# Prompt attention in a hybrid decoder step: a narrow reciprocal with copies that spread it, the scale folded into the query norm, a negated maximum, and the small units' transposes copied out by VectorE

## What is computed

```python
MLA_HEADS, MLA_NOPE, MLA_ROPE, MLA_V = 8, 64, 32, 64
MLA_SCALE = (MLA_NOPE + MLA_ROPE) ** -0.5

def _attn_block(q_lat, q_pe, q_pos, ckv, kpe, k_pos):
    s = einsum('bqhl,bkl->bhqk', q_lat, ckv) + einsum('bqhr,bkr->bhqk', q_pe, kpe)
    mask = (k_pos[None, :] <= q_pos[:, None])[None, None]
    s = where(mask, s * MLA_SCALE, NEG_INF)
    p = softmax(s, axis=-1)
    return einsum('bhqk,bkl->bqhl', p, ckv)

# in _mla_mixer
q = (_rmsnorm(cq, q_norm_g) @ w_qb).reshape(bsz, s, MLA_HEADS, MLA_NOPE + MLA_ROPE)
o = einsum('bshl,lhv->bshv', o_lat, w_uv)
```

## Time and profile before

| | |
|---|---|
| median of three runs | 3233.49 us |
| the profiled execution's own time | 3230.6 us |
| its span | 3228.9 us |
| TensorE matmul busy | 3012.1 us, 93% |
| VectorE busy | 1803.4 us, 56% |
| ScalarE busy | 944.1 us, 29% |
| mean granted TensorE clock | 0.956 |

### The profile page before, as it was taken

How to read it: one execution, slowest core, us unless ns; L and a number is a source line. 1 busy time by engine, 2 the same in 40 slices (tenths; PEclk the granted TensorE clock), 3 DMA queues, 4 the chain that set the end, 5 groups by cost and what they waited for, 6 DMA issues and landing times. The chain is left out here.

```text
span 3228.9 us, 51409 instructions
## 1 busy us (share of the span) xinstructions
PE 3012.1 (93%) x21202; PEld 2666.1 (83%) x21202; DVE 1803.4 (56%) x2982; ACT 944.1 (29%) x1550; POOL 244.4 (8%) x280
## 2 busy tenths in 40 slices
PE   6987888998999999999989779889999999999998
PEld 5975565668999999999989545556699999999998
DVE  4856677553454545444565757765535545444554
ACT  4034454553311111111220445445423111111113
POOL 2000001540000000000020000024200000000000
PEclk8986999998999999999989879999999999999998
DMA  4122102762111111111031310047421112111211
GB/s 104 46 38 55 22 5 66 252 210 68 33 53 40 51 49 53 47 40 40 23 55 34 65 39 8 11 138 236 156 62 40 54 46 58 42 40 40 59 32 67
DMA packets 226585, 207.97 MB, mean 64 GB/s; under 512 B 50260, under 2 KB 195796, under 8 KB 226148
## 3 DMA queue, kind: packets, MB, share of 16 engines
q1 hardware_dynamic: 200744, 119.38, 13.7%
q0 software_dynamic: 25600, 85.11, 8.5%
HBM read 193.58 MB, written 11.05 MB: 63 GB/s over the span
## 5 line engine op out<-in xcount | busy, mean ns | idle before, releaser
L189 PE MATMUL ps<-streamH,upH 128*128 128x344 f32 x2112 | 449.0, 321 | 6.5 <-issue 3.7
L189 PE MATMUL ps<-streamH,upL 128*128 128x344 f32 x2112 | 447.3, 320 | 0.0
L189 PE MATMUL ps<-streamL,upH 128*128 128x344 f32 x2112 | 445.9, 319 | 0.0
L2279 ACT ACTIVATE upH<-hc 128x1024 fp32r<-128x1024 f32 x88 | 93.4, 1061 | 967.9 <-PE ps L189 967.9
L189 PEld LDWEIGHTS ps<-streamH,upH 128*128 128x128 f32 x2112 | 354.4, 188 | 8.8 <-issue 4.9
L189 PEld LDWEIGHTS ps<-streamH,upL 128*128 128x128 f32 x2112 | 355.9, 188 | 0.0
L189 PEld LDWEIGHTS ps<-streamL,upH 128*128 128x128 f32 x2112 | 352.8, 188 | 0.0
L2443 DVE TENSOR_TENSOR xT<-xT,ps 128x1032 f32<-128x1032 f32 x176 | 216.0, 1228 | 227.6 <-PE ps L189 227.6
L443 PE MATMUL ps<-inH,inW 128*128 128x344 f32 (+1 forms) x1248 | 233.4, 323 | 31.3 <-DVE inW L497 31.3
L2404 DVE TENSOR_TENSOR hc<-ps,rstd 128x1032 f32<-128x1032 f32 x44 | 54.2, 1232 | 370.9 <-PE ps L189 370.9
L443 PEld LDWEIGHTS ps<-inH,inW 128*128 128x128 f32 (+1 forms) x1248 | 198.4, 183 | 38.5 <-DVE inW L497 32.3
(11 more groups left out here) (475 smaller groups left out, 4787.2 us busy)
## 6 DMA issues: line engine op xcount, KB each, us to landing
hc<-in_w_ffn_in SPq DMA_DIRECT2D x88, 512.0 KB, 4.0
hc<-in_w_ffn_out SPq DMA_DIRECT2D x44, 512.0 KB, 3.7
big<-in_w_in SPq DMA_DIRECT2D x22, 512.0 KB, 4.0
stream_raw<-in_w_out SPq DMA_DIRECT2D x16, 512.0 KB, 4.0
big<-in_x_prompt SPq DMA_DIRECT2D x2, 2048.0 KB, 10.0
out_y_prompt<-big SPq DMA_DIRECT2D x8, 512.0 KB
scratch_y<-hc SPq DMA_DIRECT2D x16, 136.0 KB, 3.4
scratch_u<-wring SPq DMA_DIRECT2D x4, 516.0 KB, 3.1
```

The costliest lines, as they stand in the source:

```text
L189: last = pe.matmul(self.ps[:, bank + n, 0:NCOL], w, x[:, n * NCOL:(n + 1) * NCOL], start=(k == 0 and i == 0), stop=(k == len(terms) - 1 an ...
L2279: act.activation(upH[u][:, :, :], raw[u], ACT.Copy).then_inc(g_wh[u], 1)
```

## The change

- `reciprocals` runs once per group of four units. It takes the reciprocal of four row sums (128x4), then spreads the four columns with two copies into 128x128 blocks, two of which now alternate between groups. It stands at the third unit of the group. ScalarE's exponential no longer waits for the reciprocal of four units before.
- The scale is folded into the reciprocal root of the query norm, as a bias of log(scale) in that Exp, so that the exponentials run without a scale. In the sample stage the factor is -1.0 instead of minus the scale.
- The row maximum is written negated, and the instruction that scaled it is gone.
- The one bank of each small unit is copied out by VectorE and no longer by ScalarE, at its true width (128 to 512 columns).
- In VectorE's loop the copy of a unit now stands ahead of `output`; it stood behind it.

```diff
+                dve.memset(self.small[:, 21:22], math.log(MLA_SCALE))
...
-        rden = [take(P) for _ in range(2)]
+        rden = [take(2 * P) for _ in range(2)]
...
-        copied_by = ["DA"[g] if u % 2 == 0 else "A" for u in range(NU) for g in range(banks_of[u])]
+        copied_by = ["DA"[g] for u in range(NU) for g in range(banks_of[u])]
...
-                    pe.wait_ge(e_r, 4 * i + 4)
+                    pe.wait_ge(e_r, i + 1)
                     for w in range(2):
-                        pe.transpose(ps[:, VALUES_BANK, (2 * w + 1) * P:(2 * w + 2) * P], rden[w], ident)
+                        pe.transpose(ps[:, VALUES_BANK, (2 * w + 1) * P:(2 * w + 2) * P], rden[i % 2][:, w * P:(w + 1) * P], ident)
...
-                    act.activation(r, r, ACT.Exp, scale=-0.5).then_inc(d_rs, 1)
+                    act.activation(r, r, ACT.Exp, scale=-0.5, bias=self.small[:, 21:22] if i else 0.0).then_inc(d_rs, 1)
...
-                    if u >= 4:
-                        act.wait_ge(e_r, u - 3)
+                    if u >= 8:
+                        act.wait_ge(e_r, u // 4 - 1)
...
-                    s.link(dve.reduce_max(slot(2, u), two[:, 0:n], AX))
                     if u >= 4:
                         dve.wait_ge(e_p, u - 3)
-                    TS(slot(0, u), slot(2, u), -MLA_SCALE, None, ALU.mult).then_inc(e_nb, 1)
-
-                def reciprocals(u):
-                    p, z, q = units[u]
-                    dve.wait_ge(e_p, u + 1)
-                    if u // 4:
-                        dve.wait_ge(e_o, u // 4)
-                    dve.reciprocal(rden[1 - u % 2][:, 64 * z:64 * z + 64], slot(1, u).to_broadcast([P, 64])).then_inc(e_r, 1)
+                    dve.reduce_max(bound(u), two[:, 0:n], AX, negate=True).then_inc(e_nb, 1)
+
+                def reciprocals(i):
+                    dve.wait_ge(e_p, 4 * i + 4)
+                    s.link(dve.reciprocal(inverse, st[:, 4 + 4 * (i % 2):8 + 4 * (i % 2)]))
+                    if i >= 2:
+                        dve.wait_ge(e_o, i - 1)
+                    for w in range(2):
+                        last = dve.tensor_copy(rden[i % 2][:, w * P:(w + 1) * P].rearrange("p (z c) -> p z c", z=2),
+                                               inverse[:, 1 - w:4 - w:2].unsqueeze(2).to_broadcast([P, 2, 64]))
+                    last.then_inc(e_r, 1)
...
-                    dve.tensor_copy(pT[1][units[u][1]][:, 0:512], ps[:, 5 + at % 2, :]).then_inc(e_te, 1)
+                    w = min(4, units[u][2] + 1) * P
+                    dve.tensor_copy(pT[1 - u % 2][units[u][1]][:, 0:w], ps[:, 5 + at % 2, 0:w]).then_inc(e_te, 1)
...
                 for u in range(NU):
                     p, v = u // NV, u % NV
+                    copies(u)
                     if u and u % 4 == 0:
                         output(u // 4 - 1)
-                    if u % 2 == 0:
-                        copies(u)
-                    reciprocals(u)
+                    if u % 4 == 2:
+                        reciprocals(u // 4)
                     if u + 3 < NU:
                         maxima(u + 3)
```

More of the change, by code:

```diff
@@ L1276, in mla_prompt @@
         small_pT = [take(512) for _ in range(2)]
-        rden = [take(P) for _ in range(2)]
+        rden = [take(2 * P) for _ in range(2)]
         rT = take(2 * P)
         wukT = W(0, 256).rearrange("p (z c) -> p z c", z=2)
-        st = W(256, 16)
+        st = W(256, 24)
         self.qs = qs = W(1024, 64).rearrange("p (b h) -> p b h", b=8)
@@ L1324, in score_banks, with bound, total @@
             return ps[:, 2 * (u // 2 % 2):2 * (u // 2 % 2) + 2, :].rearrange("p b n -> p (b n)") if u % 2 == 0 else ps[:, 4, :]
-        def slot(kind, u):
-            return st[:, 4 * kind + u % 4:4 * kind + u % 4 + 1]
+        def bound(u):
+            return st[:, u % 4:u % 4 + 1]
+        def total(u):
+            return st[:, 4 + u % 8:5 + u % 8]
+        inverse = st[:, 12:16]
         chunk = lambda c: slice(c * NCOL, (c + 1) * NCOL)
@@ L1535, in exponentials @@
                         act.wait_ge(e_t, first_bank[u - 1])
-                    if u >= 4:
-                        act.wait_ge(e_r, u - 3)
+                    if u >= 8:
+                        act.wait_ge(e_r, u // 4 - 1)
                     n = (q + 1) * P
-                    act.activation(prob[u % 2][:, 0:n], score_banks(u)[:, 0:n], ACT.Exp, bias=slot(0, u), scale=MLA_SCALE,
-                                   accum_out=slot(1, u)).then_inc(e_p, 1)
+                    act.activation(prob[u % 2][:, 0:n], score_banks(u)[:, 0:n], ACT.Exp, bias=bound(u),
+                                   accum_out=total(u)).then_inc(e_p, 1)
                 def copies(u):
@@ L1948, in exponentials @@
                         act.wait_ge(f_oc, g - 1)
-                    act.activation(alpha[g % 2], m[g % 2][1 - g // 2 % 2], ACT.Exp, bias=nb[g % 2], scale=MLA_SCALE)
+                    act.activation(alpha[g % 2], m[g % 2][1 - g // 2 % 2], ACT.Exp, bias=nb[g % 2])
                     if g >= 1:
                         act.wait_ge(f_t, order["prob", g - 1, 0] + 1)
-                    act.activation(prob, ps[:, S_BANK:S_BANK + 2, :].rearrange("p c n -> p (c n)"), ACT.Exp, bias=nb[g % 2], scale=MLA_SCALE,
+                    act.activation(prob, ps[:, S_BANK:S_BANK + 2, :].rearrange("p c n -> p (c n)"), ACT.Exp, bias=nb[g % 2],
                                    accum_out=rs[g % 2]).then_inc(f_p, 1)
@@ L2014, in bounds @@
                     s.link(TS(new, mx[0], mx[1], old, ALU.max, ALU.max))
-                    TS(nb[g % 2], new, -MLA_SCALE, None, ALU.mult).then_inc(f_nb, 1)
+                    TS(nb[g % 2], new, -1.0, None, ALU.mult).then_inc(f_nb, 1)
                 def update(g):
```

## The result

The changed kernel's median is 3217.99 us (five runs, 3213.11 to 3221.72), against 3233.49 before (3230.96 to 3234.89). The ratio is 0.9952, with a 95% interval of 0.9937 to 0.9966: faster by 15.5 us, where I had forecast +1.4. The profiled execution took 3216.33 us with a span of 3214.6, so its span is 14.3 us shorter than before's.

What follows compares the result with a forecast made beforehand. Bound: a loop of latencies between TensorE and VectorE in the prompt-attention loops. Per layer +2.18, minus 0.37, minus 1.12, together +0.7 us, +1.4 for both layers, gave 3234.9 us; own range 3230 to 3240, wider range 3221.5 to 3243.5.

Steps and rivals of the forecast that it cites:

- The moved copy: VectorE's copy ahead of `output`: delays the step after `values` from V+1.26 to V+1.96, V being when `values` is issued.
- The scaling: VectorE's scaling after each maximum: its removal saves 0.19 us, gap included, on each maximum on the path.
- Groups v = 12 to 15: Units 12 to 15 of pairs 0 to 2: step 0.41 us late, each group 0.22 us longer.
- v = 0 to 3: Units 0 to 3 in pairs 1 and 2: step 0.80 us late, each group 0.13 us longer.
- the small copy is 0.13 shorter than the last reciprocal: End of group v = 4 to 7: copy replaces the reciprocal ahead of `values`, which starts 0.24 us later.
- pair 3: Last pair, without steps, so late `output` holds nobody: groups gain 0.32, 0.34, 0.32 and 0.14 us, 1.12 a layer.
- +0.18: Group v = 8 to 11, pairs 0 to 2: step 0.61 us late, each group 0.18 us longer.
- the first group of pair 0: Units 0 to 3 of pair 0, with no `output` ahead: 0.37 us shorter.
- The wait before them stays, so I leave them: TensorE's half-clock stretches in v = 8 to 11, two a layer, some 1.5 us each, were forecast to remain.
- the first rival: Prompt-attention loops: step not held, VectorE's lighter load reaches TensorE in full; 12 us gained, 3221.5 us; chance 0.22.
- The second (nothing made up): Prompt-attention loops: the held step's delay is not made up by VectorE's saving; 5.3 us a layer, 3244 us; chance 0.18.
- The third, TensorE's clock: Half-clock stretches in v = 8 to 11: all four gone gives 6 us less, 3229; four more, 6 more; chance 0.10.

Runs made afterwards that it cites:

- output_first: The changed kernel with only the order undone, VectorE running `output` ahead of the unit's bank copy again: 3208.27 us, ratio 0.9924.
- transposes_late: The changed kernel with TensorE, in `values`, waiting for the bank copies first and transposing the reciprocals after: 3221.62 us, ratio 0.9966.
- swap_only: The kernel before the change with only VectorE's bank copy moved ahead of `output`: 3249.46 us, ratio 1.0046.
- look2: Changed kernel with small units' copies back on ScalarE, `output` first again, maxima two units ahead, not three: 3233.26 us (3196.11 without the maxima edit).
- max_only: The kernel before the change with only the negated maximum and the folded scale, also in the sample stage: 3217.01 us, ratio 0.9956.
- copies_only: The kernel before the change with only the small units' copies moved to VectorE at true width: 3259.75 us, ratio 1.0083.

## Why the prediction was wrong

*Right.* TensorE idles for the chain, not for VectorE's load: output_first, transposes_late, swap_only and look2 keep VectorE's load and move the time by 10, 4 (9 by the groups), 16.5 and 37 us. All durations held. The moved copy costs what I said in kind: step at V+1.77 where I had V+1.96, and undoing it gains 10 us. The scaling is worth 0.19 us on each maximum of v = 4 to 7, 8 to 11 and 12 to 15, shown in max_only. Groups v = 12 to 15 (+0.13, forecast +0.22) and v = 0 to 3 (+0.18, forecast +0.13) came within 0.1 us.

*The step that failed first: "the small copy is 0.13 shorter than the last reciprocal (382.89). `values` (383.59) starts 0.24 us later".* I let the whole of `values` wait for the copy that took the reciprocal's place. But in the code that I had before me, `values` transposes the reciprocals before it waits for the copies. With the reciprocal moved to the third unit, these transposes are no longer behind VectorE's last instruction: they fill TensorE's wait. transposes_late takes just this back and measures 0.38 to 0.39 us in each v = 4 to 7 and v = 8 to 11 and in the last two groups of pair 3. Together with the step 0.19 earlier than in my walk (the copy starts 0.05 earlier, and 0.06 us pass from `output` to the step in place of 0.20), it turns +0.24 into -0.29 and +0.18 into -0.42. Six such groups a layer are 3 x 0.53 + 3 x 0.60 = 3.4 us; pair 3 adds 1.3 (2.46 gained, 1.12 forecast; 0.8 of it is the transposes again, by transposes_late, the other 0.5 was not traced to a cause), the first group of pair 0 takes 0.35 away (forecast -0.37, measured -0.02), v = 12 to 15 and v = 0 to 3 make 0.2. That is 4.5 us a layer, 9 in all.

*The second: "The wait before them stays, so I leave them" (the half-clock stretches).* The wait of 1.80 us before `values` in v = 8 to 11 became 1.35, with two transposes done ahead of it, and all four stretches went: 2.9 and 3.0 us. I had this as a rival of its own with 0.10, when it hangs in part on the same thing as the group times: with the transposes behind the wait again (transposes_late) TensorE stands still there for 1.61 us, and one stretch a layer is back. A shorter wait is not all of it, since max_only has 1.62 us and kept two a layer. Added to the first rival's 12 us the 6 us would have opened the range to 3215.5; taken apart, the range ended at 3221.5, 3.5 us short of the result.

The two make 15 of the 15.7 us between +1.4 and the profile's -14.3; the rest lies outside the stretches.

*What I did not see at all* is that the change holds one large gain and two losses. I weighed the small units' copies by their durations, and found them equal to the reciprocals that they replace; compared with the kernel before that is so. Compared with leaving them on ScalarE, they put the last thing that `values` needs back behind VectorE's queue, and spend 9 to 13 us of what the reciprocal gave. My own sentence that ScalarE has 96 us to spare said as much. The Trainium skill (VectorE: DVE Perf Modes, Specifications) places ScalarE closer to PSUM; the traces agree, with 0.05 us more a copy on VectorE (288 to 685 ns against 277 to 597). The loss by queue is larger: 9 to 13 us over 64 copies, 0.15 to 0.2 us each.

*The rivals.* The first (VectorE's relief reaches TensorE) came nearest in number, 3221.5, but not by its mechanism: the step was held all the same. Without the hold the time is 3208. The second (nothing made up) is swap_only's case, and there it was dearer than I had it, for the clock. The third, TensorE's clock, was right in its size, 5.9 us of the 6, and came on top of the rest.

## What to carry to other kernels

In a loop of engines that wait for one another, an instruction's worth is not its length but whether someone waits at its end: taking the last reciprocal out of the place ahead of `values`, and making it narrow, gained 30 us, and copies put into that place lost 9 to 13 of them, though VectorE still had less to do than before. When work is moved between engines, ask which queue the last operand of the waiting instruction now comes out of, and leave it with the engine that is idle then. And walk the waiting engine's own code to the first wait: what stands ahead of it is hidden, what stands behind it is paid.

## What the hardware showed that I had not expected

The clock multiplied small waits. Before, with a wait of 1.80 us ahead of `values`, two of three groups v = 8 to 11 a layer ran their matmuls at 1.2 GHz, at 1.5 us each; with 1.35 us (changed) there were none, and with 2.39 us (copies_only) all of them were affected and took 16.4 to 17.3 us. In swap_only 5.2 us more of idle time came with 17.7 us more of busy time. The Trainium skill (TensorE: Matmul & The Clock Gate, What's actually happening) says that the gate follows how busy the engine was of late; these runs agree, with granted clocks of 1.00 (changed, no such stretch), 0.98 (before) and 0.94 (swap_only). But the length of that one wait does not decide it. At 1.61 us (transposes_late) one group of three fell, that of pair 1; at 1.62 (max_only) two, those of pairs 0 and 1; at 1.80 two before, those of pairs 1 and 2, and all three in swap_only, where the wait before `values` was the same 1.80. What decides between pairs with the same waits was not tried and stays open.
